# Both remaining attentions beside tile 0's expert slots, both query stages after them, and the second half of the slots alone

## What is computed

```
h = x + W_out [ MLA(xn) | DSA(xn) ],   xn = RMSNorm(x), one input projection W_in
h = h + PEER(RMSNorm(h));              y = RMSNorm_final(h)
MLA: latent attention, 8 heads, key rows of 256 + 32
DSA: indexer scores, top-k keys (64 of 256 for the prompt, 256 of 1028 for the sample), softmax with a bias
PEER: q = xn W_pq; per head the best 16 of 128 keys twice, the best 16 of their sums,
      then for each of the 8 heads x 16 chosen experts:  out += gate * gelu(u[e] . xn) * v[e]
```

## Time and profile before

| | us |
|---|---|
| median of 3 runs | 1014.88 |
| the profiled execution, first to last instruction (span) | 1080.4 |
| tile 0's front, and slots 0 to 39 | 0 to 245 |
| tile 1's attention and output projection | 245 to 430 |
| tile 1's query product and choice | 430 to 556 |
| the sample's attention and output projection | 556 to 905 |
| the sample's query product and choice | 905 to 991 |
| slots 256 to 287 and the end | 991 to 1080 |

### The profile page before, as it was taken

How to read it: one execution, slowest core, us unless ns; L and a number is a source line. 1 busy time by engine, 2 the same in 40 slices (tenths; PEclk the granted TensorE clock), 3 DMA queues, 4 the chain that set the end, 5 groups by cost and what they waited for, 6 DMA issues and landing times.

```text
span 1080.4 us, 13828 instructions
## 1 busy us (share of the span) xinstructions
PE 742.8 (69%) x4217; PEld 379.1 (35%) x4217; DVE 686.7 (64%) x1725; ACT 404.0 (37%) x1154; POOL 622.1 (58%) x584
## 2 busy tenths in 40 slices
PE   8999986554798677766536768757637567765444
PEld 3575834111354435543212233323213235231111
DVE  1363776997288543698695559988974535639542
ACT  1162142332356470333223346354516742322412
POOL 0000275777667765475565656766775665667664
PEclk9999997877778899988867878877778878887656
DMA  9924699999979999999899999999998999999997
GB/s 364 331 79 184 217 349 411 411 360 377 336 252 359 348 400 412 398 379 379 278 314 325 373 388 353 391 362 362 407 412 308 411 417 416 414 411 409 382 376 270
DMA packets 122443, 381.54 MB, mean 353 GB/s; under 512 B 16026, under 2 KB 40682, under 8 KB 117122
## 3 DMA queue, kind: packets, MB, share of 16 engines
q0 software_dynamic: 83696, 304.81, 74.0%
q1 hardware_dynamic: 38578, 75.78, 19.2%
q10 hardware_dynamic: 96, 0.07, 0.0%
HBM read 378.16 MB, written 4.14 MB: 354 GB/s over the span
## 4 chain that ended last, share of the span: by engine, by line
PE 28%; DVE 19%; issue 17%; ACT 10%; another core or an unknown queue 9%; DMA 8%; POOL 6%; SPq 3%; ACTq 0%; POOLq 0%; DVEq 0%
PE bank L463 17%; PE acc L463 9%; DVE rows L1453 6%; DMA w_uq_sb<-in_w_uq 3%; PE bank L466 3%; POOL rows L1978 3%; DMA rows<-in_peer_v,eid 2%; POOL rows L1996 2%; ACT spread L1101 2%; ACT L1092 1%; SPq L2069 1%; DVE shared L1793 1%; DVE shared L1782 1%; ACT shared L1063 1%
## 5 line engine op out<-in xcount | busy, mean ns | idle before, releaser
L463 PE MATMUL acc<-rows,spread 128*64 128x512 f32 (+1 forms) x1124 | 329.3, 682 | 143.9 <-ACT spread L1101 51.9
L1978 POOL DMA_INDIRECT rows<-in_peer_v,eid x254 | 275.8, 1086 | 160.5 <-issue 66.6
L1996 POOL DMA_INDIRECT rows<-in_peer_u,eid x184 | 193.2, 1050 | 109.0 <-issue 54.7
L463 PEld LDWEIGHTS acc<-rows,spread 128*64 128x64 f32 (+1 forms) x1124 | 89.1, 156 | 310.3 <-issue 240.2
L1453 DVE CUSTOM_DVE_ANT_0 rows<-rows,xr_even 128x1024 f32<-128x1024 f32 x89 | 108.1, 1218 | 34.0 <-DMA rows<-in_peer_u,eid 26.4
L1453 DVE CUSTOM_DVE_ANT_0 rows<-rows,xr_odd 128x1024 f32<-128x1024 f32 x95 | 116.2, 1223 | 19.6 <-DMA rows<-in_peer_u,eid 18.8
L1101 ACT ACTIVATE spread<-wide_consts,wts 128x64 f32<-128x64 f32 (+1 forms) x288 | 83.7, 337 | 35.2 <-remote 25.0
L1996 POOL DMA_INDIRECT first_u<-in_peer_u,eid x37 | 38.2, 1032 | 101.5 <-DVE eid L1835 81.6
L463 PE MATMUL acc<-more_v,spread 128*64 128x512 f32 (+1 forms) x140 | 73.6, 695 | 18.9 <-ACT spread L1101 9.9
L1094 ACT ACTIVATE wts<-gelus,gate 128x1 f32<-128x1 f32 x288 | 69.1, 287 | 4.7
L1063 ACT ACTIVATE shared<-bank 128x512 f32<-128x512 f32 (+4 forms) x68 | 27.8, 456 | 76.3 <-remote 35.5
(11 more groups left out here) (278 smaller groups left out, 1222.4 us busy)
## 6 DMA issues: line engine op xcount, KB each, us to landing
wring<-in_w_pq SPq DMA_DIRECT2D x12, 1024.0 KB
z<-in_w_pq SPq DMA_DIRECT2D x5, 1024.0 KB, 4.8
wring<-in_cache_ckv SPq DMA_DIRECT2D x40, 128.0 KB
rows<-in_w_in SPq DMA_DIRECT2D x2, 2048.0 KB, 15.2
rows<-in_w_pq SPq DMA_DIRECT2D x2, 2048.0 KB, 8.3
wring<-in_w_out SPq DMA_DIRECT2D x4, 1024.0 KB
wring<-in_cache_kv SPq DMA_DIRECT2D x32, 128.0 KB
rows<-in_peer_v,eid POOLq DMA_INDIRECT x254, 7.5
```

Of the source, the lines that this page charges most:

```text
L463: return T.matmul(o, lhsT=l, rhs=r, start=start, stop=stop, skip_group_check=True)
L1978: nc.gpsimd.indirect_dma_start(out=v_ring[V_PLACE[n]], out_offset=None, in_=inp["peer_v"], in_offset=bass.IndirectOffsetOnAxis(ap=eid[t][: ...
L1996: nc.gpsimd.indirect_dma_start(out=u_ring[U_PLACE[n]], out_offset=None, in_=inp["peer_u"], in_offset=bass.IndirectOffsetOnAxis(ap=eid[t][: ...
```

## The change

The fronts of tiles 1 and 2 are cut in two. First come both attentions with their output projections and norms, tile 1's beside slots 40 to 65 and the sample's beside slots 66 to 113; then tile 1's query product and choice beside slots 114 to 127, and the sample's beside slots 128 to 143. Slots 144 to 287 have no front beside them. Tile 1's `xn2` waits in the ring buffer `more_u`, which takes no slot from 50 to 137, the sample's in `qq_t`; the first guest buffer leaves at slot 84. `index_pages(0)` stands behind tile 1's second output product, and the `w_pq` chunks of both tiles behind all pages and `w_out` chunks. The finish of tile 0 moves behind tile 1's choice.

```diff
-FRONT = 5 * W_IN + 4 * W_HEADS + 8 * W_PQ + 16 * CHOOSE
-
-SHARES = [16 * CHOOSE, FRONT + 12 + 9 * W_PROMPT, FRONT - 8 * CHOOSE + 3 * W_INDEX + 2 * STEPS * sum(W_MID.values())]
+FRONT = 5 * W_IN + 4 * W_HEADS
+
+SHARES = [16 * CHOOSE, FRONT + 12 + 9 * W_PROMPT, FRONT + 3 * W_INDEX + 2 * STEPS * sum(W_MID.values()),
+          8 * W_PQ + 16 * CHOOSE, 8 * W_PQ + 8 * CHOOSE]
-U_GUESTS = [(24, 118), (144, sum(SLOTS) - 1)]
+KEPT_FROM, KEPT_TO = 50, 138
+U_GUESTS = [(24, 84), (144, sum(SLOTS) - 1)]
...
-    places = [*range(RU), *(RU + i for i, (a, b) in enumerate(U_GUESTS) if a <= n <= b)]
+    places = [*(p for p in range(RU) if p != 1 or not KEPT_FROM <= n < KEPT_TO), *(RU + i for i, (a, b) in enumerate(U_GUESTS) if a <= n <= b)]
...
-FIRST_SLOT = [0, EARLY, 128, 256]
+FIRST_SLOT = [0, EARLY, 66, 114, 128, 144]
...
-        xn2 = mix_f
+        xn2 = [mix_f, more_u, qq_t[0:32, :, :].rearrange("p h n -> p (h n)")]
...
-        CHUNKS = [(t, w, c) for t in (1, 2) for w, n in (("out", 4), ("pq", 8)) for c in range(n)]
+        CHUNKS = [(t, w, c) for w, n in (("out", 4), ("pq", 8)) for t in (1, 2) for c in range(n)]
...
+            for t in (1, 2):
+                experts.front(t + 2)
+                for c in range(4):
+                    share(W_PQ)
+                    share(W_PQ)
+                    if t == 1:
+                        best_keys(t, 2 * c, 2, ("sc", c, t))
+                        choose(t, c, lambda: share(CHOOSE))
+                    elif c % 2:
+                        best_keys(t, c // 2, 1, ("sc", c // 2, t))
+                        choose(t, c // 2, lambda: share(CHOOSE))
+                if t == 1:
+                    experts.rest(BASE[1])
+                    replicate(1, range(PAIR))
+                    experts.rest(BASE[1] + 6)
+                    finish(0)
+                    experts.rest(BASE[1] + 10)
+            experts.rest(BASE[2])
+            replicate(2, [0])
+            experts.rest(BASE[2] + 6)
+            finish(1)
+            experts.rest(N_SLOTS)
             finish(2)
...
-            chunks(1, "pq", 0, 3, PRELOADED)
+            page_of.extend(page_id(slice(i, i + 1)) for i in range(GB * NPG))
             logits_sb.wait(sp, ("d", 1, HG[1] - 1))
...
-            chunks(1, "pq", 3, 8, PRELOADED)
-            ready(sp, ("pq", 2, 1))
+            ready(sp, ("wo", 1, 1))
             index_pages(0)
-            ready(sp, ("pq", 3, 1))
             index_pages(1)
             step_pages("m", 0)
-            output(0)
...
             chunks(2, "out", 3, 4)
+            chunks(1, "pq", 0, 8)
             chunks(2, "pq", 0, 8)
+            output(0)
             output(1)
```

More of the change, by code:

```diff
@@ L97 @@
 STAIR = 16 + 15 * 8
-FIRST_SLOT = [0, EARLY, 128, 256]
+FIRST_SLOT = [0, EARLY, 66, 114, 128, 144]
+U_AGAIN = min(n for n in range(KEPT_TO, N_SLOTS) if U_PLACE[n] == 1)
+U_KEPT = max(n for n in range(KEPT_FROM) if U_PLACE[n] == 1)
 def free(ap, *dims):
@@ L427, in __init__, with front, due, closer @@
                 self.log = handovers[name] = []
-            def front(self, t):
-                self.t, self.weight = t, 0
+            def front(self, stage):
+                self.stage, self.weight = stage, 0
             def share(self, w):
-                if self.t:
+                if self.stage:
                     self.advance(w)
+            def due(self):
+                first, end = FIRST_SLOT[self.stage:self.stage + 2]
+                return first + (end - first) * self.weight // SHARES[self.stage]
             def advance(self, w):
                 self.weight += w
[L438 to L441, removed]
-                while self.n < until:
[L443 to L453, removed]
+                self.log.append((self.stage, w))
+                assert self.weight <= SHARES[self.stage], (self.stage, self.weight)
+                self.rest(self.due() - self.lag)
+            def closer(self, lag):
+                self.rest(self.due() - lag)
+            def rest(self, until):
+                while self.n < until:
+                    self.slot(max(t for t in tiles if BASE[t] <= self.n), self.n)
                     self.n += 1
@@ L555, in transpose_x @@
                     b = take(pe, (what, t, c))
-                    src = x_in_sb[t] if what == "x" else xn2
+                    src = x_in_sb[t] if what == "x" else xn2[t]
                     for j in range(4):
@@ L1024, in _ @@
                     read_done(pe, ("x2", 0, 0))
[L1025 to L1047, removed]
+                    read_done(pe, ("x2", 0, 1))
+                    first_query_product()
+                    next_tiles_z(1, 6, 8)
+                    for q in (2, 3):
+                        z_product_of_sample(q)
+                    for c in range(1, 4):
+                        query_product(c, 0)
+                        if c == 2:
+                            next_tiles_z(2, 0, 8)
+                            next_tiles_z(3, 0, 8)
+                            for i in range(6):
+                                experts.advance(CHOOSE)
                     for i in range(10):
@@ L1050, in _ @@
                 else:
-                    experts.rest(t - 1)
-            experts.rest(2)
+                    share(W_IN)
+            for t in (1, 2):
+                experts.front(t + 2)
+                experts.closer(4)
+                xn2_ready.wait(pe, t)
+                transpose_x(t, "x2")
+                read_done(pe, ("x2", t, 1))
+                for c in range(4):
+                    query_product(c, t)
+                    if t == 1 or c % 2:
+                        for i in range(4):
+                            share(CHOOSE)
+                if t == 1:
+                    experts.rest(BASE[1])
+            experts.rest(N_SLOTS)
             y_square.wait(pe, 2)
@@ L1438, in _ @@
                             keep_z1(3)
-            experts.rest(2)
+            for t in (1, 2):
+                experts.front(t + 2)
+                x_evac("x2", t)
+                for c in range(4):
+                    share(W_PQ)
+                    queries(c, t)
+                    share(W_PQ)
+                    if t == 2 and c % 2 == 0:
+                        continue
+                    share(CHOOSE)
+                    share(CHOOSE)
+                    gate_exps(t, c // t)
+                    share(CHOOSE)
+                    share(CHOOSE)
+                if t == 1:
+                    experts.rest(BASE[1])
+                    y_root(0)
+                    experts.rest(BASE[1] + 4)
+            experts.rest(BASE[2])
+            y_root(1)
+            experts.rest(N_SLOTS)
             y_root(2)
@@ L1442, in _ @@
             for q in (2, 3):
-                act.dma_start(out["y_s"][:, 256 * q:256 * q + 256], xn2[32 * q:32 * q + 32, 0:256]).then_inc(y_out, 16)
+                act.dma_start(out["y_s"][:, 256 * q:256 * q + 256], yn[32 * q:32 * q + 32, 0:256]).then_inc(y_out, 16)
         @block.vector
@@ L1508, in finish @@
                     dve.wait_ge(g_fin_in, 16)
+                if t == 1:
+                    dve.wait_ge(y_out, 16)
                 if t == 2:
@@ L1914, in _ @@
                                             free(g_ffn_turned[:, 0:1], (1, 4), (0, 128)), ALU.mult), ("x2", 0, 0))
-                rms(x[t][0:n, :], g_ffn[0:n, :], xn2[0:n, :], ("h", t), xn2_ready, t)
+                if t == 1:
+                    dve.wait_ge(dots_done, U_KEPT + 1)
+                rms(x[t][0:n, :], g_ffn[0:n, :], xn2[t][0:n, :], ("h", t), xn2_ready, t)
                 share(W_IN)
[L1917 to L1928, removed]
+                for c in range(0 if t else 4):
+                    if c:
                         best_keys(t, 2 * c, 2, ("sc", c, t))
@@ L1939, in _ @@
                         choose(t, 1, lambda: experts.advance(CHOOSE))
[L1940 to L1946, removed]
+            for t in (1, 2):
+                experts.front(t + 2)
+                for c in range(4):
+                    share(W_PQ)
+                    share(W_PQ)
+                    if t == 1:
+                        best_keys(t, 2 * c, 2, ("sc", c, t))
[3 more added lines that the diff above has]
+                        choose(t, c // 2, lambda: share(CHOOSE))
+                if t == 1:
+                    experts.rest(BASE[1])
+                    replicate(1, range(PAIR))
+                    experts.rest(BASE[1] + 6)
+                    finish(0)
+                    experts.rest(BASE[1] + 10)
+            experts.rest(BASE[2])
+            replicate(2, [0])
+            experts.rest(BASE[2] + 6)
+            finish(1)
+            experts.rest(N_SLOTS)
             finish(2)
             assert handovers["PE"] == handovers["Activation"] == handovers["DVE"]
-            for t in (1, 2):
+            for t in range(1, len(SHARES)):
                 assert sum(w for u, w in handovers["DVE"] if u == t) == SHARES[t], (t, sum(w for u, w in handovers["DVE"] if u == t))
@@ L1993, in _ @@
```

(8 more changed lines are left out.)

43 lines of the change are left out of this document (8 added, 35 removed).

## The result

The changed kernel takes 1177.84 us (median, 1170.89 to 1182.00), the kernel before 1015.04 beside it: a ratio of 1.161, 95% interval 1.158 to 1.164. It is 163 us slower. The forecast was 1145 us, in a range of 1070 to 1200.

The account below looks back on a forecast made before the run. Loads, at a 409 GB/s ceiling, were taken to bound the kernel from 245 us on. Stage terms 245 + 130 + 90 + 128 + 66 + 20 + 92 + 72 + 376 = 1219 us, times 0.939, gave 1145 us; range 1070 to 1200.

Parts of the forecast that it names:

- The price of a slot alone: Slots with no front beside them: 2.56 us each at 409 GB/s; the whole stage 376 us.
- Tile 1's attention: Stage with 26 slots beside it: 130 us, between 108 with TensorE never idle and 145.
- tile 1's choice: Tile 1's query and choice with 14 slots: 92 us, between VectorE's 76 and 101.
- the sample's choice: Tile 0's finish and the sample's query and choice, 16 slots: 72 us, between 62 of loads and 86.
- The index pages: Sample's attention up to its first m step: SyncE's page issues hold it up, 90 us, between 79 and 97.
- The m steps: Eight steps of the sample's attention with 24 slots: 128 us, VectorE's own work and slots together 122.
- The d steps: Eight steps of the sample's attention with 12 slots, a chain across engines: 66 us, between 51 and 80.
- The ring costs nothing: Six u buffers in slots 85 to 137: no cost, as the quota by weight holds loads back there.
- the scale: Last step: the 1219 us sum times 0.939, runs over profiled span (1014.88 / 1080.4), giving 1145 us.
- The fronts did not shrink to their busiest engine: Rival for the front stages: with fewer slots they run as fast as VectorE's work, 322 us; total 935 us; 5%.
- The page rival: Rival for the sample's stretch to its first m step: pages cost little, 45 us; total 1103 us; 14%.
- the slow-slots rival: Rival for slots alone: ring and chain too short for the ceiling, 424 us, not 376; total 1190 us; 16%.

Follow-up runs that it names:

- before_cover_of_after: Kernel before in its old order, with only the changed kernel's slot numbers beside each front (40 and 64), the other slots alone: 1126.78 us, ratio 1.112.
- after_choice_48: Changed kernel with slots 128 to 175 beside the sample's query and choice instead of 128 to 143, and 112 slots alone: 1172.16 us, ratio 1.155.

## Why the prediction was right, and what in it was not

- *The loads are the bound and the change takes their cover away.* Right, and shown by `before_cover_of_after`: the old order with the new numbers of slots makes 113 of the 163 us. The price of a slot alone held: 2.56 us was forecast, and 180 us at 409 GB/s were measured; the stage took 380 against 376. TensorE waits there for v rows, as it should when the loads are the bound (800 to 1160 us):

```profile
PE acc L467 <- DMA rows<-in_peer_v,eid: 148.1, 67, 3.7
```

- *Tile 1's attention* 124 against 130, *tile 1's choice* 84 against 92, *the sample's choice* 64 against 72: TensorE and VectorE are the bounds that the prediction gave the first two (98 of 124 us and 73 of 84 us busy), and each waits a little less than I took. The third runs at 355 GB/s, below the ceiling; that it has little room left rests on `after_choice_48`.
- *The index pages.* The mechanism held: 67 us of issues and 79 us to the first m step, which was the lower bound. The 90 lay between it and an upper bound, 97, from the stretched issues of the first recording. By the Trainium skill (DMA: Bandwidth & Descriptors, Issuing engines are not separate DMA queues) the issues would usually be small beside the transfers; 67 us for 2.1 MB, and 39 us gained by dropping half, speak against that for transfers of 32 KB.
- *The m steps* took 134 against 128: VectorE is busy for 122, as summed. *The d steps* 61 against 66.
- *The ring costs nothing*: not contradicted, but tested only by one buffer fewer. The reason given was put too simply: the loads do wait for buffers, which come free at the quota's pace.
- *The step that failed is the last one, the scale.* The sum in profiled time was 1219, the profiled time 1180. I multiplied by 0.939, since the first recording was longer than the runs by that. But after's recording is not longer than its runs (1179.8 and 1177.84), and neither is a second one of before. So the sum was 39 us too high, part of it because its terms came from stretched rows, and the scale took off 74 us that were not there. The two errors point in opposite directions and leave 33 us. Without the scale, the sum would have been 41 us high. That the forecast came as close as 33 us, and lay in its range, is thus in part luck: 1219 us is above the range.
- *The rivals.* The fronts did not shrink to their busiest engine: 245 us to the end of tile 1's choice was to take below 387 us for it, and took 496. The page rival (45 us) and the slow-slots rival (424 us) are off by 33 and 44 us, though the total of the latter, 1190, lies nearer to the result than mine. "No effect" is out.
- *The signs.* The rounds come every 17 us a step (134 / 8), close to the 16 forecast, and the slots alone run at 409 GB/s. The front stages have 167 to 415 GB/s and not 250 to 300. The sign of TensorE's clock failed: below 0.83 was to be seen in the first stages, and tile 1's attention has 0.92 (0.95 before, second recording); only behind it, up to the first m step, does it fall to 0.67, where TensorE is busy for 38 of 78 us.

Of the 163 us, 113 are cover. The other 50 belong to what the new order adds. Half of the page issues are worth 39 in after; before, they lie beside tile 1's choice at 393 GB/s, and no run took them out there. How the rest divides was not separated; the lower clock in some of the new stages and the ring's seventh buffer are not excluded as parts of it.

## What to carry to other kernels

When loads are the bound, ask of a reordering only whether they stay busy: count the bytes that stand beside each stage, divide by the ceiling, and compare with the stage's own chain. A stage whose chain is longer loses the difference for good, since work without a front beside it can't run faster than the ceiling. Before scaling from a profiled time to a run's, record once more: a span that differs from the runs by 6% may be that recording's own.

## What was not expected of the hardware

- One recording of an unchanged program was 1080.4 us and the next 1010.1, with runs at 1012 to 1016. In the first, 64 instructions of SyncE followed one another in 0.69 to 0.72 us, against 4 in the second and 4 in after's trace. What stretched the first is not known.
- 409 GB/s from HBM stood for 180 us on end. The limit of about 358 GB/s for loads from HBM (the Trainium skill, DMA: Bandwidth & Descriptors, Where 436 GB/s comes from) did not bind this kernel, which uses one core; the section works it out as half of what a stack of HBM gives two cores.
